# Branch projections of a conv/gMLP/MoE step in split weights and inputs, with their loads and the modulation loads on one queue

## The chip, the cores and the metric

One Trainium2 chip, one core of it. The number is the device time of one execution in microseconds. Three runs of the kernel before took 975.2, 977.08 and 981.87 us; the median is 977.08.

The engines, as the profile names them: PE (TensorE, matrix products; PEld is its weight load), DVE (VectorE), ACT (ScalarE), POOL (GpSimd), SP (SyncE, which here only issues DMAs; SPq is its DMA queue).

## The reference, cut to what matters

One inference step of one layer for 512 prompt tokens and 32 sample tokens (T = 544 together), model width D = 1024, all float32.

```
mod = silu(c) @ w_ada + b_ada            # 6 vectors of D: sh1 sc1 g1 sh2 sc2 g2
h = rms_norm(x) * (1 + sc1) + sh1
z = h @ w_in + b_in                      # conv input a (2D), u, v (D each), gates (2D)
a = silu(layer_norm(depthwise_conv(glu(a))));   y_a = a @ w_a
v = layer_norm(gelu(v));   y_b = (gelu(u) * (w_s mixes v over positions)) @ w_b
m = sigmoid(gate_a) * y_a + sigmoid(gate_b) * y_b
x = x + g1 * (m @ w_o)
h2 = rms_norm(x) * (1 + sc2) + sh2;   x = x + g2 * experts(h2);   final norm with its own mod
```

The change is in `y_b`, `y_a` (two products of 544 x 1024 by 1024 x 1024) and in what is loaded from there to the output projection.

## The kernel before

Everything is one program with one instruction stream per engine, written out by hand; semaphores order the streams. In most stages the activations lie transposed: 128 channels on the partitions, the 544 tokens along the row, 8 such tiles for D (`KT` = 8).

**Stages.** Conv input and v projection; u projection (`U_U`, 4 units); gates (`U_G`, 8 units, 16 output tiles); branch projections (`U_YB`, `U_YA`; 16 output tiles, the first 8 are `uT` by w_b, the other 8 `aT` by w_a); output projection (`U_O`); routing; experts. The weights of all these go through two buffers of 16 KB a partition, `W[0]` and `W[1]`, used in turn. The same two places are called `WP[s]` when a unit of only 2 x 128 output columns is loaded; then `wH2[s]` and `wL2[s]` are its halves. `w_used` counts the units that TensorE has finished, `w_full` the loads that landed.

**Two kinds of product.** `product` (L511 to L518) gives one output tile of 128 x 544: for each of 8 k, two float32 matmuls of 272 columns; in the trace each of these is two records. `product_split` (L577 to L583) gives the same tile from operands split in two parts, each in the type float32r: high (the value rounded to it) and low (the rest). It makes three products for each k: high weights by high input, high by low, low by high; 48 matmuls of 272 columns, each one record. The u projection and the gates are done so, the branch projections in `product`.

**Who splits.** ScalarE copies the weights of a unit to `wH2` (`high_of`, L961 to L964). POOL subtracts that from the weights (`low_gate`, L1631 to L1634; VectorE does it for the u projection) and writes `wL2`, over the place of the loaded weights. `gH`, `gL` are the split input of the gates; `gL` lies where `x` lay (`O_X`).

**Branch stage.** For output tile j, TensorE waits for the weights (`full`) and for the PSUM banks that merge(j-2) has drained, then makes `product`. VectorE's `merge(j)` (L1307 to L1322) multiplies the result by a gate and, for j >= 8, adds it to the first branch in `mT`. In between, TensorE makes 12 small products of the conditioning with 512 columns of w_ada or w_ada_f (`ada(m)`, L684 to L693, after tile m + 3), each from a 2 MB load into `AW[m % 2]`. VectorE's `add_bias(m)` (L1324 to L1333) sums four partial rows and the bias, POOL writes the row to `mod` in HBM and loads the bias row of m + 2. ada(m) waits for add_bias(m-2). POOL issues all these loads (`load_mod`, `load_bias`).

**SP's queue.** It loads the units in order, each when `w_used` frees its buffer; between w_b and w_a it loads `x` a second time, since L1359 adds to it. After w_o it loads the vectors g1, sc2 (`g1b`, `a2b`), g_norm2 (`gn2b`), sh2 (`sh2b`) and then the first experts' weights.

**Output projection.** TensorE makes token blocks 0 and 1 with the first half of w_o, then waits for the second half (L726 and on). VectorE (L1342 to L1368) multiplies by g1, adds x, norms and modulates to h2, which TensorE transposes block by block.

Of the kernel before, what the change touches and what calls it, by code (L numbers as in the profile page):

```python
# [31 lines left out]
P = 128  # L32
D = 1024
# [38 lines left out]
def build(nc, a, y_out, hist_p_out, hist_s_out, v_out):  # L72
    with ExitStack() as ctx:
# [21 lines left out]
        gH, gL = split_parts("gH", O_S, KT, T), split_parts("gL", O_X, KT, T)  # L95
        wH2 = [split_parts(f"wH2{s}", O_W + 4096 * s + 2048, 2, KT, P) for s in range(2)]
# [130 lines left out]
        x2_in = sem("x2_in")  # L227
        u_split = sem("u_split")
        bias_split, conv_sum = sem("bias_split"), sem("conv_sum")
# [146 lines left out]
        U_A, U_V, U_U, U_G, U_YB, U_YA, U_O = 4, 12, 14, 18, 26, 28, 30  # L376
# [3 lines left out]
        NB = 12  # L380
# [18 lines left out]
        def _(sp):  # L399
# [11 lines left out]
            def unit_load(n, cols):  # L411
                sp.wait_ge(w_used, n - 1 if n >= U_A + 2 else n - 3)
                for m in range(2):
                    sp.dma_start(WP[n % 2][:, m], w_in[:, :, cols[m]:cols[m] + P]).then_inc(w_full[n % 2], 16)
# [21 lines left out]


            for p in range(2):
                sp.wait_ge(mod_stored[p], 16 * 3)
            for s, rows in ((0, P), (1, NSAMPLE)):  # L440
                g_rows = P if s == 0 else 2 * NSAMPLE
                sp.dma_start(g1b[s][0:g_rows, :], mod_vec(2, g_rows, s)).then_inc(mb_in, 16)
                sp.dma_start(a2b[s][0:rows, :], mod_vec(4, rows, s)).then_inc(mb_in, 16)
            sp.wait_ge(mod_added, NB)
            sp.dma_start(gn2b, a["g_norm2"].to_broadcast([P, D])).then_inc(mb2_in, 16)
            sp.wait_ge(dve_drained, KT + NGATE)
            for s, rows in ((0, P), (1, NSAMPLE)):
                sp.dma_start(sh2b[s][0:rows, :], mod_vec(3, rows, s)).then_inc(mb2_in, 16)

# [60 lines left out]
        def _(pe):  # L510
# [66 lines left out]
            def product_split(bank, w_high, w_low, act_high, act_low):  # L577
# [121 lines left out]
            for j in range(NGATE):  # L699
                n = U_YB + j // 4  # L700
                if j % 4 == 0:
                    full(pe, n)
                if j == KT:
                    pe.wait_ge(a_ready, 2 * KT)
                if j >= 2:
                    pe.wait_ge(dve_drained, KT + j - 1)
                last = product(2 * (j % 2), W[n % 2][:, :, (j % 4) * P:(j % 4 + 1) * P], uT if j < KT else aT)
                last.then_inc(w_used if j % 4 == 3 else y_ps, 1)
# [178 lines left out]
        def _(act):  # L887
# [237 lines left out]
        def _(dve):  # L1125
# [180 lines left out]

            def merge(j):  # L1307
                b, n = j % 2, U_YB + j // 4
                m_j = two(mT[:, j % KT, :])
                if j % 4 == 3:  # L1310
                    dve.wait_ge(w_used, n + 1)
                else:
                    dve.wait_ge(y_ps, 3 * (j // 4) + j % 4 + 1)
# [35 lines left out]
            for t in range(TT):  # L1349
# [8 lines left out]
                dve.wait_ge(o_drained, 2 * t + 2)  # L1358
                dve.tensor_tensor(x[0:w, t, :], x[0:w, t, :], mg[0:w, :], ALU.add).then_inc(x1_ready, 1)  # L1359
# [3 lines left out]
                if t >= 2:  # L1363
# [3 lines left out]
                                              op0=ALU.mult, op1=ALU.mult))  # L1367
                dve.tensor_tensor(h2[0:w, t % 2, :], h2[0:w, t % 2, :], sh2b[s][0:w, :], ALU.add).then_inc(h2_ready, 1)  # L1368
# [230 lines left out]
        def _(pool):  # L1599
# [55 lines left out]
            def mod_of(m):  # L1655
                return (w_ada, a["b_ada"], (4 + m) * BLK) if m < 8 else (w_adaf, b_adaf, (m - 8) * BLK)

            def load_mod(m):
                src, bias, c0 = mod_of(m)
                pool.dma_start(AW[m % 2], src[:, :, c0:c0 + BLK]).then_inc(mod_in[m % 2], 16)  # L1660

            def load_bias(m):
                src, bias, c0 = mod_of(m)
                pool.dma_start(brow[:, m % 2, :], bias[:, c0:c0 + BLK].to_broadcast([2, BLK])).then_inc(bias_in[m % 2], 16)

# [89 lines left out]
```

## Time and profile before

| | |
|---|---|
| median of three runs | 977.08 us |
| profiled execution | 976.06 us, its span 974.3 us |
| PE busy | 862.8 us, 89% of the span |
| DVE, ACT, POOL busy | 495.0, 168.1, 150.1 us |
| branch products and adas | 415.2 to 557.5 us |
| output projection | from 559.2 us |

The span is what the profiler saw from first to last instruction; some 1.8 us lie around it. "Busy" of PE counts matmuls, which overlap each other, so full means that it always had one in work, not that it ran at its peak. PEclk is the clock granted to TensorE as a share of 2.4 GHz: 1.00 is 2.4, 0.50 is 1.2. An idle time in brackets at the end of a timeline row stands before the instruction and names what ended it.

### The profile page before, as it was taken

How to read it: one execution, taken by the hardware profiler on the slowest of the kernel's cores; microseconds unless marked ns; L12 is line 12 of the kernel's file. 1: busy time of each engine (PE TensorE's matmuls, PEld its weight loads, DVE VectorE, ACT ScalarE, POOL GpSimd, SP SyncE). 2: the span in 40 equal slices, each digit the busy share in tenths (PEclk: the TensorE clock that was granted, in tenths of full speed). 3: DMA queues.
4: the chain of work that ended last, by engine and by line, in shares of the span. 5: the costliest groups of instructions: out<-in, count | busy, mean ns of one | idle time of the engine just before them, and what ended most of it. 6: DMA issues, size and time to landing. Idle time of an engine off the chain costs nothing. (4 is left out here: it accounts for less than half of the span.)

```text
span 974.3 us, 11529 instructions
## 1 busy us (share of the span) xinstructions
PE 862.8 (89%) x4738; PEld 613.3 (63%) x4738; DVE 495.0 (51%) x734; ACT 168.1 (17%) x255; POOL 150.1 (15%) x176
## 2 busy tenths in 40 slices
PE   2899999999997979899999999926999996979776
PEld 1588886347996979877666644524666664545432
DVE  1429999999999543301434425472333332222226
ACT  3211211111232121800000012100211110101003
POOL 1000000000056273201112000001222222121110
PEclk9899999999998889999999999955999998999889
DMA  9913214012323124275778392162899999999926
GB/s 321 326 47 87 80 50 173 1 43 66 90 67 96 39 55 153 102 264 196 261 276 307 101 385 99 48 259 76 357 397 419 418 415 390 374 408 396 379 105 255
DMA packets 94709, 204.12 MB, mean 210 GB/s; under 512 B 10028, under 2 KB 52372, under 8 KB 86462
## 3 DMA queue, kind: packets, MB, share of 16 engines
q1 hardware_dynamic: 69200, 134.10, 37.9%
q0 software_dynamic: 12624, 34.32, 9.6%
q10 hardware_dynamic: 12830, 34.93, 9.3%
q8 instruction: 39, 0.64, 0.3%
q14 instruction: 16, 0.13, 0.0%
HBM read 199.49 MB, written 14.84 MB: 220 GB/s over the span
## 5 line engine op out<-in xcount | busy, mean ns | idle before, releaser
L517 PE MATMUL PS<-arena 128*128 128x272 f32 x1024 | 240.9, 397 | 3.5 <-issue 1.9
L517 PEld LDWEIGHTS PS<-arena 128*128 128x128 f32 x1024 | 195.0, 191 | 53.8 <-issue 13.8
L1236 DVE SCALAR_TENSOR_TENSOR arena<-arena,VT 128x574 f32<-128x574 f32 x240 | 175.2, 818 | 0.0
L824 PE MATMUL PS<-arena 128*64 128x256 f32 (+1 forms) x1056 | 148.2, 410 | 29.9 <-issue 25.8
L824 PEld LDWEIGHTS PS<-arena 128*64 128x64 f32 (+1 forms) x1056 | 108.1, 156 | 65.4 <-issue 38.7
L582 PE MATMUL PS<-gH,wH 128*128 128x272 f32 x384 | 82.1, 296 | 9.2 <-POOL wL L1634 5.6
L1634 POOL TENSOR_TENSOR wL<-arena,wH 128x1024 fp32r<-128x1024 f32 x16 | 40.9, 2582 | 271.1 <-ACT wH L964 271.1
L582 PE MATMUL PS<-gL,wH 128*128 128x272 f32 x384 | 81.2, 293 | 0.0
L582 PE MATMUL PS<-gH,wL 128*128 128x272 f32 x384 | 80.9, 292 | 0.0
L1530 DVE TENSOR_TENSOR arena<-PS,arena 128x256 f32<-128x256 f32 x19 | 8.1, 425 | 139.5 <-ACT arena L1070 139.5
L844 PE MATMUL PS<-arena 128*64 128x512 f32 (+1 forms) x264 | 69.1, 597 | 1.4 <-DVE arena L1534 1.4
L582 PEld LDWEIGHTS PS<-gH,wH 128*128 128x128 f32 x384 | 61.4, 193 | 11.2 <-POOL wL L1634 5.8
L582 PEld LDWEIGHTS PS<-gH,wL 128*128 128x128 f32 x384 | 61.9, 193 | 0.0
L582 PEld LDWEIGHTS PS<-gL,wH 128*128 128x128 f32 x384 | 61.6, 193 | 0.0
L1710 POOL DMA_INDIRECT pairs<-arena,sidx x19 | 30.6, 1613 | 191.4 <-DVE arena L1546 191.4
L718 PE MATMUL PS<-arena 128*128 128x512 f32 x128 | 55.5, 593 | 1.7 <-DVE arena L1322 1.7
L619 PE MATMUL PS<-arena 128*128 128x512 f32 x128 | 56.2, 592 | 0.0
L1050 ACT ACTIVATE tmp<-arena 128x1024 f32<-128x1024 f32 (+1 forms) x6 | 6.3, 1058 | 222.1 <-DVE arena L1359 202.8
L844 PEld LDWEIGHTS PS<-arena 128*64 128x64 f32 (+1 forms) x264 | 22.6, 145 | 34.0 <-issue 32.5
L718 PEld LDWEIGHTS PS<-arena 128*128 128x128 f32 x128 | 24.1, 190 | 31.2 <-issue 31.2
L1070 ACT ACTIVATE arena<-PS 128x256 f32<-128x256 f32 x19 | 7.3, 385 | 209.1 <-PE PS L824 209.1
L619 PEld LDWEIGHTS PS<-arena 128*128 128x128 f32 x128 | 24.3, 190 | 29.0 <-issue 28.8
(275 smaller groups left out, 811.3 us busy)
## 6 DMA issues: line engine op xcount, KB each, us to landing
arena<-w_gate SPq DMA_DIRECT2D x32, 1024.0 KB
arena<-w_up SPq DMA_DIRECT2D x32, 1024.0 KB
arena<-w_down ACTq DMA_DIRECT2D x28, 1024.0 KB, 15.5
arena<-w_in SPq DMA_DIRECT2D x40, 512.0 KB, 5.2
arena<-w_ada SPq DMA_DIRECT2D x4, 2048.0 KB, 20.6
vecs<-w_ada POOLq DMA_DIRECT2D x4, 2048.0 KB, 9.5
arena<-w_ada POOLq DMA_DIRECT2D x4, 2048.0 KB, 8.5
arena<-x_prompt SPq DMA_DIRECT2D x8, 512.0 KB, 10.5
```

The lines of the kernel that those rows point to most:

```text
L517: last = pe.matmul(PS[:, bank + h, 0:H], tile_w[:, k, :], act[:, k, h * H:(h + 1) * H], start=(k == 0), stop=(k == KT - 1))
L582: last = pe.matmul(PS[:, bank + h, 0:H], w[:, k, :], part[:, k, h * H:(h + 1) * H], start=(k == 0 and n == 0), stop=(k == KT - 1 and n == 2))
L619: last = pe.matmul(PS[:, bank, :], hT[:, k, t * P:(t + 1) * P], W[hf][:, k, :], start=False, stop=(k == KT - 1))
L718: last = pe.matmul(PS[:, (2 * t + hf) % 8, :], mT[:, k, t * P:(t + 1) * P], W[hf][:, k, :], start=(k == 0), stop=(k == KT - 1))
L824: last = pe.matmul(PS[h * rows:(h + 1) * rows, 2, n * DE:(n + 1) * DE], hG[:, b, k * SLOTS + h * rows:k * SLOTS + (h + 1) * rows], buf[r / ...
L844: last = pe.matmul(PS[h * rows:(h + 1) * rows, 4 + 2 * b + hf, :], heT[:, k, h * rows:(h + 1) * rows], WD[r // 2][r % 2][:, k, hf * 512:(h ...
L1050: act.activation(scratch[0:w, :], src, ACT.Square, accum_out=ss[0:w, t:t + 1]).then_inc(act_step, 1)
L1070: act.activation(sil, PS[:, 2, 0:DE], ACT.Silu).then_inc(sil_ready, 1)
L1236: dve.scalar_tensor_tensor(out=total, in0=src, scalar=tap, in1=total, op0=ALU.mult, op1=ALU.add).then_inc(conv_step, 1)
L1530: dve.tensor_tensor(he, PS[:, 2, DE:2 * DE], sil, ALU.mult).then_inc(he_ready, 1)
L1634: pool.tensor_tensor(wL2[q % 2][:, m], WP[q % 2][:, m], wH2[q % 2][:, m], ALU.subtract).then_inc(gw_split, 1)
L1710: pool.indirect_dma_start(out=pairs, out_offset=bass.IndirectOffsetOnAxis(ap=sidx[b][:, 0:1], axis=0), in_=Y[:, b, :], in_offset=None, bou ...
```

## The change

The branch projections are made with `product_split`. Their weights come in 8 units of 256 columns instead of four halves of 512; units are split by ScalarE and POOL as in the gates (POOL's `low_gate` now runs to unit 16). The inputs are split too: `yH` is the high part (at `O_X`, where `gL` was), `uL` and `aL` are written over `uT` and `aT`. For u the first three high parts are copied by VectorE, the other five by ScalarE; for a all eight by ScalarE. VectorE makes the low parts; those of a stand before merge(7) in its stream. TensorE waits per k for them in tiles 0 and 8. ScalarE's `high_of(U_YB)` stands before the last two gate drains. All modulation and bias loads and the `mod` stores move from POOL's queue to SP's, among the unit loads. g1 and sc2 are loaded within the branch stage; x (whose place yH now has) after the second half of w_o, its parts each with the semaphore of its first load, VectorE waiting per token block; sh2 is waited for only at the first block's last step.

```diff
+        yH, uL, aL = split_parts("yH", O_X, KT, T), split_parts("uL", O_U, KT, T), split_parts("aL", O_C, KT, CONV)
...
-        U_A, U_V, U_U, U_G, U_YB, U_YA, U_O = 4, 12, 14, 18, 26, 28, 30
+        U_A, U_V, U_U, U_G, U_YB, U_YA, U_O = 4, 12, 14, 18, 26, 30, 34
-        NB = 12
+        NB, EARLY = 12, 3
...
-            for n, (src, c0) in enumerate(((w_b, 0), (w_b, BLK))):
-                half_load(U_YB + n, src, c0)
-            for t in range(4):
-                sp.dma_start(x[:, t, :], a["x_prompt"][0, t * P:(t + 1) * P, :]).then_inc(x2_in, 16)
-            sp.dma_start(x[0:NSAMPLE, 4, :], a["x_sample"][0]).then_inc(x2_in, 16)
-            for n, (src, c0) in enumerate(((w_a, 0), (w_a, BLK), (w_o, 0), (w_o, BLK))):
-                half_load(U_YA + n, src, c0)
+            def branch_load(q):
+                unit_load(U_YB + q, [(2 * (q % 4) + m) * P for m in range(2)], w_b if q < 4 else w_a)
...
+            branch_load(0)
+            branch_load(1)
+            sp.wait_ge(gated, KT)
+            load_mod(0)
+            sp.wait_ge(w_used, U_YB)
+            load_mod(1)
+            load_bias(0)
+            load_bias(1)
+            for j in range(NGATE):
+                if j % 2 == 1 and j // 2 + 2 < 8:
+                    branch_load(j // 2 + 2)
+                if 3 <= j < 3 + NB - 2:
+                    sp.wait_ge(mod_ps, j - 2)
+                    load_mod(j - 1)
+                if 4 <= j < 4 + NB:
+                    m = j - 4
+                    sp.wait_ge(mod_added, m + 1)
+                    sp.dma_start(mod[:, (4 + m) * BLK:(5 + m) * BLK], mrow[:, m % 2, :]).then_inc(mod_stored[m % 2], 16)
+                    if m + 2 < NB:
+                        load_bias(m + 2)
+                if j == 12:
...
+                if j == 13:
+                    half_load(U_O, w_o, 0)
+            sp.dma_start(gn2b, a["g_norm2"].to_broadcast([P, D])).then_inc(gn_in, 16)
+            half_load(U_O + 1, w_o, BLK)
+            for t in range(2):
+                sp.dma_start(x[:, t, :], a["x_prompt"][0, t * P:(t + 1) * P, :]).then_inc(x_in[t], 16)
             sp.wait_ge(dve_drained, KT + NGATE)
...
...
                 for k in range(KT):
+                    if split is not None:
+                        pe.wait_ge(y_split, split + k + 1)
...
             for j in range(NGATE):
-                n = U_YB + j // 4
-                if j % 4 == 0:
-                    full(pe, n)
-                if j == KT:
-                    pe.wait_ge(a_ready, 2 * KT)
+                q, m = j // 2, j % 2
+                pe.wait_ge(gw_split, NGATE + j + 1)
                 if j >= 2:
                     pe.wait_ge(dve_drained, KT + j - 1)
-                last = product(2 * (j % 2), W[n % 2][:, :, (j % 4) * P:(j % 4 + 1) * P], uT if j < KT else aT)
+                last = product_split(2 * m, wH2[q % 2][:, m], wL2[q % 2][:, m], yH, uL if j < KT else aL, j if j % KT == 0 else None)
...
+            high_of(U_YB)
             gate(NGATE - 2)
             gate(NGATE - 1)
+            for j in range(EARLY, KT):
+                act.activation(yH[:, j, :], uT[:, j, :], ACT.Copy).then_inc(y_high, 1)
+            for n in range(1, 5):
+                high_of(U_YB + n)
+            act.wait_ge(w_used, U_YA)
+            for j in range(KT):
+                act.activation(yH[:, j, :], aT[:, j, 0:T], ACT.Copy).then_inc(y_high, 1)
+            for n in range(5, 8):
+                high_of(U_YB + n)
...
+            def low_of(first, before, src, dst):
+                for j in range(first, KT):
+                    dve.wait_ge(y_high, before + j - first + 1)
+                    dve.tensor_tensor(dst[:, j, 0:T], src[:, j, 0:T], yH[:, j, :], ALU.subtract).then_inc(y_split, 1)
...
+            dve.wait_ge(gated, KT)
+            dve.wait_ge(w_used, U_YB)
+            for j in range(EARLY):
+                dve.tensor_copy(yH[:, j, :], uT[:, j, :]).then_inc(y_copied, 1)
+                dve.wait_ge(y_copied, j + 1)
+                dve.tensor_tensor(uL[:, j, 0:T], uT[:, j, 0:T], yH[:, j, :], ALU.subtract).then_inc(y_split, 1)
+            low_of(EARLY, 0, uT, uL)
             dve.wait_ge(gate_drained, NGATE)
             for j in range(NGATE):
+                if j == KT - 1:
+                    dve.wait_ge(a_ready, 2 * KT)
+                    low_of(0, KT - EARLY, aT, aL)
                 merge(j)
...
-            dve.wait_ge(x2_in, 16 * TT)
             dve.wait_ge(mb_in, 64)
-            dve.wait_ge(mb2_in, 48)
+            dve.wait_ge(gn_in, 16)
...
+                dve.wait_ge(x_in[t], 32)
+                if t == 0:
+                    dve.wait_ge(mb2_in, 32)
...
-            for q in range(4, 8):
+            for q in range(4, 16):
                 low_gate(q)
...
```

## Rows read from the trace of the kernel before

**Rows 1.** Windows: stretch, length, busy PE, PEld, DVE, ACT, POOL; PEclk, DMA share, GB/s.
```profile
415.20:557.50 142.30, 142.28 (x704) 101.09 (x704) 45.05 (x66) 0.00 (x0) 19.68 (x31) 1.00 0.65 238
...
380.00:386.00 6.00, 6.00 (x50) 6.00 (x50) 0.00 (x0) 2.57 (x3) 4.75 (x2) 1.00 0.00 0
```

**Rows 2.** Timeline of PE (start, us, line, count): branch products, adas, output projection.
```profile
415.22 10.09 PE L517 MATMUL PS<-arena 128*128 128x272 f32 x43 [1.91 <-issue]
...
444.72 1.92 PE L692 MATMUL PS<-vecs 128*32 128x512 f32 x16
...
454.11 1.92 PE L692 MATMUL PS<-arena,vecs 128*32 128x512 f32 x16
...
559.17 27.70 PE L718 MATMUL PS<-arena 128*128 128x512 f32 x64 [1.67 <-DVE arena L1322]
```

**Rows 3.** Timeline of DVE in the branch stage: two merges, add_bias's last three steps.
```profile
437.50 0.72 DVE L1316 TENSOR_TENSOR arena<-PS,arena 128x544 f32<-128x544 f32 x1 [6.61 <-PE PS L517]
444.83 0.72 DVE L1316 TENSOR_TENSOR arena<-PS,arena 128x544 f32<-128x544 f32 x1 [6.61 <-PE PS L517]
...
550.25 2.13 DVE L1331 TENSOR_TENSOR mrow<-PS,mrow 2x512 f32<-2x512 f32 x3
```

**Rows 4.** Timelines of SPq and ACT: a gate unit's load and split, gate drains.
```profile
374.08 0.99 SPq L414 DMA_DIRECT2D arena<-w_in  x2
...
379.96 2.01 ACT L964 ACTIVATE wH<-arena 128x1024 fp32r<-128x1024 f32 x2 [5.15 <-DMA arena<-w_in]
...
386.20 0.71 ACT L1006 ACTIVATE arena<-PS,VT 128x544 f32<-128x544 f32 x1 [3.63 <-PE PS L582]
...
412.40 1.28 ACT L1006 ACT_TABLE_LOAD   x1
413.69 1.32 ACT L1006 ACTIVATE arena<-PS,VT 128x544 f32<-128x544 f32 x2
```

**Rows 5.** Timelines of POOL and DVE: low weights, one DVE product beside them.
```profile
271.69 7.45 POOL L1634 TENSOR_TENSOR wL<-arena,wH 128x1024 fp32r<-128x1024 f32 x2 [246.53 <-ACT wH L964]
...
313.47 9.30 POOL L1634 TENSOR_TENSOR wL<-arena,wH 128x1024 fp32r<-128x1024 f32 x4
...
318.47 4.89 DVE L1296 TENSOR_TENSOR arena<-arena,tmp 128x544 f32<-128x544 f32 x1
...
393.08 4.75 POOL L1634 TENSOR_TENSOR wL<-arena,wH 128x1024 fp32r<-128x1024 f32 x2 [7.24 <-ACT wH L964]
```

**Rows 6.** Timeline of PE, then a window, after the longest idle gap in gates.
```profile
359.96 0.82 PE L582 MATMUL PS<-gH,wH 128*128 128x272 f32 x2 [5.56 <-POOL wL L1634]
...
362.00:364.00 2.00, 2.00 (x11) 2.00 (x11) 1.97 (x2) 0.18 (x1) 2.00 (x3) 0.52 0.03 8
```

**Rows 7.** Groups by form: count, busy us, mean ns of one.
```profile
L1242 DVE TENSOR_TENSOR gL<-arena,gH 128x544 fp32r<-128x544 f32 x8 | 5.2, 726 | 0.0
...
L960 ACT ACTIVATE gH<-arena 128x544 fp32r<-128x544 f32 x8 | 4.9, 673 | 0.0
```

**Rows 8.** Windows (columns of Rows 1); DMA issues: KB each, median us to landing.
```profile
10.00:20.00 10.00, 2.83 (x16) 0.68 (x16) 1.61 (x3) 7.04 (x12) 0.00 (x0) 1.00 1.08 338
...
366.00:368.00 2.00, 2.00 (x18) 2.00 (x18) 2.00 (x1) 0.00 (x0) 2.00 (x2) 1.00 1.02 410
...
386.00:392.00 6.00, 6.00 (x47) 5.79 (x46) 0.00 (x0) 0.77 (x2) 0.00 (x0) 1.00 0.64 175
...
vecs<-w_ada POOLq DMA_DIRECT2D x4, 2048.0 KB, 9.5
...
arena<-w_o SPq DMA_DIRECT2D x2, 1024.0 KB, 6.5
...
arena<-mod SPq DMA_DIRECT2D x2, 128.0 KB, 10.7
```

**Rows 9.** Timelines of SPq and DVE at the head of the output projection.
```profile
561.80 0.35 SPq L445 DMA_DIRECT2D arena<-g_norm  x1
...
580.04 0.69 DVE L1357 TENSOR_TENSOR tmp<-PS,arena 128x512 f32<-128x512 f32 x1 [2.55 <-PE PS L718]
```

More of the change, by code:

```diff
@@ L226, in build @@
         w_full = [sem("w_full0"), sem("w_full1")]
-        x2_in = sem("x2_in")
+        gn_in = sem("gn_in")
         u_split = sem("u_split")
+        y_high, y_copied, y_split = sem("y_high"), sem("y_copied"), sem("y_split")
         bias_split, conv_sum = sem("bias_split"), sem("conv_sum")
@@ L433, in mod_vec, with mod_of, load_mod, load_bias @@
+            def mod_of(m):
+                return (w_ada, a["b_ada"], (4 + m) * BLK) if m < 8 else (w_adaf, b_adaf, (m - 8) * BLK)
+            def load_mod(m):
+                src, bias, c0 = mod_of(m)
+                sp.dma_start(AW[m % 2], src[:, :, c0:c0 + BLK]).then_inc(mod_in[m % 2], 16)
+            def load_bias(m):
+                src, bias, c0 = mod_of(m)
+                sp.dma_start(brow[:, m % 2, :], bias[:, c0:c0 + BLK].to_broadcast([2, BLK])).then_inc(bias_in[m % 2], 16)
             def mod_vec(n, rows, s):
@@ L434, in mod_vec @@
                 return mod[s:s + 1, n * D:(n + 1) * D].to_broadcast([rows, D])
[L438 to L445, printed above, removed]
+            branch_load(0)
@@ new lines, in _ @@
+            branch_load(1)
[18 more added lines that the diff above has]
+                if j == 12:
+                    sp.wait_ge(w_used, U_YA)
+                    for p in range(2):
+                        sp.wait_ge(mod_stored[p], 16 * 3)
+                    for s, rows in ((0, P), (1, NSAMPLE)):
+                        g_rows = P if s == 0 else 2 * NSAMPLE
+                        sp.dma_start(g1b[s][0:g_rows, :], mod_vec(2, g_rows, s)).then_inc(mb_in, 16)
+                        sp.dma_start(a2b[s][0:rows, :], mod_vec(4, rows, s)).then_inc(mb_in, 16)
+                if j == 13:
+                    half_load(U_O, w_o, 0)
@@ L448, in _ @@
                 sp.dma_start(sh2b[s][0:rows, :], mod_vec(3, rows, s)).then_inc(mb2_in, 16)
+            for t in range(2, 4):
+                sp.dma_start(x[:, t, :], a["x_prompt"][0, t * P:(t + 1) * P, :]).then_inc(x_in[t], 16)
+            sp.dma_start(x[0:NSAMPLE, 4, :], a["x_sample"][0]).then_inc(x_in[4], 16)
             sp.wait_ge(hist_ps, 2)
@@ L575, in _, with product_split @@
             pe.wait_ge(ws_copied, 1)
-            def product_split(bank, w_high, w_low, act_high, act_low):
+            def product_split(bank, w_high, w_low, act_high, act_low, split=None):
                 for k in range(KT):
+                    if split is not None:
+                        pe.wait_ge(y_split, split + k + 1)
                     for n, (w, part) in enumerate(((w_high, act_high), (w_high, act_low), (w_low, act_high))):
@@ L699, in _ @@
             for j in range(NGATE):
[L700 to L704 removed]
+                q, m = j // 2, j % 2
+                pe.wait_ge(gw_split, NGATE + j + 1)
                 if j >= 2:
                     pe.wait_ge(dve_drained, KT + j - 1)
[L707 to L708 removed]
+                last = product_split(2 * m, wH2[q % 2][:, m], wL2[q % 2][:, m], yH, uL if j < KT else aL, j if j % KT == 0 else None)
+                last.then_inc(w_used if m == 1 else y_ps, 1)
                 if 3 <= j < 3 + NB:
@@ L1304, in _ @@
                 dve.tensor_tensor(cv[:, j, :], cv[:, j, :], rstdc[:, :], ALU.mult).then_inc(c_normed, 1)
+            def low_of(first, before, src, dst):
+                for j in range(first, KT):
+                    dve.wait_ge(y_high, before + j - first + 1)
+                    dve.tensor_tensor(dst[:, j, 0:T], src[:, j, 0:T], yH[:, j, :], ALU.subtract).then_inc(y_split, 1)
             def merge(j):
-                b, n = j % 2, U_YB + j // 4
+                b, n = j % 2, U_YB + j // 2
                 m_j = two(mT[:, j % KT, :])
-                if j % 4 == 3:
+                if b == 1:
                     dve.wait_ge(w_used, n + 1)
                 else:
-                    dve.wait_ge(y_ps, 3 * (j // 4) + j % 4 + 1)
+                    dve.wait_ge(y_ps, j // 2 + 1)
                 y = PS[:, 2 * b:2 * b + 2, 0:H]
@@ L1653, in _ @@
                 pool.tensor_tensor(sq[:, j, :], cv[:, j, :], cv[:, j, :], ALU.mult).then_inc(squared, 1)
[L1655 to L1664, printed above, removed]
-            for q in range(4, 8):
-                low_gate(q)
-                if q == 4:
-                    pool.wait_ge(gated, KT)
-                    load_mod(0)
-                    load_bias(0)
-                    load_bias(1)
-            pool.wait_ge(w_used, U_YB)
-            load_mod(1)
-            for m in range(NB):
-                if m + 2 < NB:
-                    pool.wait_ge(mod_ps, m + 1)
-                    load_mod(m + 2)
-                pool.wait_ge(mod_added, m + 1)
-                pool.dma_start(mod[:, (4 + m) * BLK:(5 + m) * BLK], mrow[:, m % 2, :]).then_inc(mod_stored[m % 2], 16)
-                if m + 2 < NB:
-                    load_bias(m + 2)
+            for q in range(4, 16):
+                low_gate(q)
             pool.wait_ge(tokens_known, 1)
```

4 lines of the change are left out of this document (2 added, 2 removed).

## The prediction

> **What bounds the kernel now.** I read the windows of the stage that changes first, then the timelines inside it and around its two ends. Between 415.2 and 557.5 us TensorE is busy 142.28 of 142.30 us at full clock, VectorE 45, ScalarE 0, the DMA engines 65% [rows 1]: the branch stage is bound by TensorE alone, and any saving there moves the end. The reader should see a beat in [rows 2]: one 128x544 product in full float32, then one 512-column modulation product (`ada`), every 9.39 us. Before the first ada VectorE's merges start 7.33 us apart [rows 3]. So a product costs 7.33 and an ada 2.06: 16 x 7.33 + 12 x 2.06 = 142.0, which is the stage. The gates, done as three products of split operands each, take 12.1 us a unit of two, from 374.08 (its predecessor's end lets a load go) to the drain at 386.20, so 6.06 each [rows 4], and there TensorE and its weight load are both full [rows 1].
>
> **The products.** Removed: 16 products of 7.33. Added: 16 of 48 matmuls, of the gates' own shape, at 6.06. That is 16 x 1.27 = **20.3 us** gained. Ada keeps its 2.06. 6.06 us is 126 ns a matmul, each with its own weight load, in the same instruction as the new ones will be, so I take it. The Trainium skill (TensorE: Matmul & The Clock Gate, section Back-to-back issue gap) gives a lone matmul columns over 2.4 GHz plus 2.5 ns, which for 272 columns is an estimated 116 ns; by it a product would be 5.56 us and the gain 28; the trace's gates don't agree.
>
> **Getting the weights split.** In the gates a 1 MB unit (two loads) is issued at 374.08, is in ScalarE's hands at 379.96 (5.9 later), takes 2.01 for both high parts and 4.75 for both low parts on POOL, of which TensorE waits for the first half [rows 4, 5]: 5.9 + 1.0 + 2.4 = 9.3 us. A buffer is refilled when its unit ends; the next unit covers 12.1 us without ada, 12.1 + 3 x 2.06 = 18.3 with. Both exceed 9.3, so units 1 to 7 cost nothing. If that cover went, each would cost the shortfall.
>
> **The hand-over from gates to branches, term 1.** ScalarE is done with its second group of Silu at 412.4, loads a table and drains gates 14 and 15 by 415.01; the products start 0.2 later [rows 2, 4]. The new `high_of(U_YB)` stands before those drains: +2.01. TensorE still waits for all 16 drains, so it may start at 417.2 instead of 415.2: **2.0 us** lost.
>
> **The hand-over, term 2.** gL's place becomes yH, so no high part of u can be written before the last gate ends at 413.3 (415.22 less 1.91 idle). VectorE then makes three copies and differences; in the same microseconds POOL makes the first two low weights, from 413.4 (first high part) to 418.2. A VectorE difference of this size takes 0.73 us [rows 7], but a product of that size with both inputs in SBUF, begun while POOL worked on low weights, took 4.89 and ended 0.6 after POOL's run [rows 5]. So I take the first difference as done at 418.9, not 414.8. TensorE then has been idle 5.6 us; after the idle 5.56 us before 359.96 it ran at the 1.2 GHz level to 364, 11 matmuls in two microseconds where full clock gives 18 by the same count [rows 6, 8], 0.228 us apart instead of 0.126. From 419.0 three of the eight k steps (six matmuls each) then take 1.37 and five take 0.76: 7.9 us, end 426.9. VectorE keeps ahead of this (a copy at most as long as a difference, 0.73, and differences 5.2 / 8 = 0.65 apart), and ScalarE's five copies at 4.9 / 8 = 0.61 from 417.0 are ready by 420.1 [rows 7]. Without either effect product 0 would end at 423.3: **3.6 us** lost. Bounds: 0 (POOL and VectorE miss each other) and 6.3 (POOL takes 7.45 for its pair beside a busy VectorE, as once [rows 5]). Early copies on VectorE thus buy little; ScalarE's come soon after.
>
> **The middle.** At product 8 the same yH is refilled from aT. ScalarE starts when product 7 ends (T), VectorE's first difference is ready at T + 1.5, ada(4) covers until T + 2.06, and eight differences 0.65 apart stay ahead of k steps of 0.76 [rows 7]. But merge(7) and add_bias(3) now stand behind the eight differences: merge ends near T + 6.8, add_bias, four steps of 2.13 / 3 [rows 3], at T + 9.6. ada(5) needs it at T + 8.1: **1.5 us** lost. Bounds 0 and 4. Later a merge's second step (two SBUF inputs) can meet POOL's low weights: at most 4.2 late, against a slack of 8.1 - 4.4 = 3.7, so under half a microsecond for each of three units; I count nothing.
>
> **The loads.** All adas and biases move from POOL's queue to SP's, in one order with the units. SP waits for product end, ada end, add_bias end, in the order in which these happen, so no wait holds up an earlier need. Per two products: one unit and two 2 MB ada loads, 5.24 MB in 16.2 us, 323 GB/s. A backlogged queue moved 338 GB/s at the kernel's start and 410 in an ada load alone, so 2 MB are 5.2 us; in the six microseconds of a unit's load the DMA engines were busy 0.64, 3.8 us [rows 8]. So 3.8 + 2 x 5.2 = 14.2 of 16.2 us: tight, but it fits, and an ada load has 14 us from issue to need against 9.5 to land. Bias loads and `mod` stores now sit behind a 2 MB load, some 6 us; a bias has 12 from issue to need. POOL's freed issue time had no waiter.
>
> **The output projection.** The second half of w_o was issued as the last product ended; now it stands behind add_bias(11), whose end let gn2b go 4.3 us after the products [rows 9], and behind gn2b itself. It landed 6.5 after issue; with the later issue and 0.5 MB ahead, that is end + 13.4. TensorE needs it at end + 1.7 + 27.7 / 2 = 15.5 [rows 2, 8]. Hidden with 2 us to spare; at the 10.7 of a neighbouring load it would cost 1. x is queued right behind (2.6 us for each MB) and needed only when the first row block's second half is in, 22.5 after the end [rows 9]. VectorE's wait for the vectors goes, but what is late next, the product at 580.04, bounds it, so nothing is gained. After that all is as before: the experts' first loads go out some 3 us later with over 60 to spare.
>
> **Sum.** 20.3 - 2.0 - 3.6 - 1.5 = 13.2. The profiled execution took 976.06 (span 974.3), so 962.9; the median of the three, 977.08, stands 1.0 above it. I predict **963 us**.
>
> **Rivals.** (1) Free hand-overs: only the ScalarE term stays, gain 18.3, 958 (957 if that too hides). For it: POOL may finish before VectorE asks. Against: the 4.89 us row. 0.17. (2) The matmuls follow each other faster than in the gates. A full float32 matmul is two records of 235 ns (43 in 10.09 us [rows 2]); if each is two passes, a pass of 272 columns takes 117 ns, and at that pace a product is 5.63: 7 us more, 956. Against: the gates, same shape, same engine state, keep 126. 0.03. The page named above would have it so. (3) Loads on one queue reach about 300 GB/s: 17.5 instead of 16.2 per pair, five pairs, 6 us worse, 970. For it: 65% DMA before becomes 80 to 90, and the old stage moved only 238 GB/s [rows 1]; against: it had no backlog. 0.14. (4) Slower than before: the same queue under 271 GB/s (5.24 MB per 19 us) would have each ada wait for mod_in and eat the 13.2; under about 249, 21 us per pair, it ends over 1% slower, 988 or so. It decides only if mixing 512-byte with 2 KB pieces costs a third of the rate; no row shows a backlogged queue that slow for more than a microsecond or two. 0.06. Forecast: 0.60.
>
> **Numbers.** 1% (what can be told from no change) is 9.8 us: below 967.3 is faster. Forecast with its bounds runs 959 to 968, nine tenths of it below: 0.56 + 0.17 + 0.03 = 0.76 faster; 0.04 + 0.14 = 0.18 same; 0.06 slower. The range 955 to 971 takes in rivals 1 and 2 and most of 3.
>
> **What would show it.** Products: pairs of units 16.2 us apart, sum of PE windows 20 us shorter. Term 1: last gate sigmoid near 417.0. Term 2: first VectorE difference ending near 418.9 and the clock at half in the first 4 us of products. Middle: one TensorE wait of 1.5 us for mrow before the sixth ada. Loads: no wait of TensorE for mod_in or for a low weight. It is wrong if TensorE waits on DMA in the stage, if a product is not 6.06, or if a wait appears before the second half of w_o.

## The result, and the profile after

| us | before | after |
|---|---|---|
| median of four runs each, same chip | 978.89 | 965.97 |
| lowest and highest | 975.2 to 981.87 | 963.69 to 970.1 |
| profiled execution (its span) | 976.06 (974.3) | 964.99 (963.2) |

The ratio is 0.989, 95% interval 0.9856 to 0.9923: a gain clear of noise, though the interval takes in 0.99, where the prediction drew its line for "faster". At the medians it is 12.9 us, between the two profiled executions 11.1; the forecast sum was 13.2.

Busy time in the page of the kernel after, which answers to the table before:

```profile
PE 845.6 (88%) x4994; PEld 618.5 (64%) x4994; DVE 509.0 (53%) x753; ACT 190.9 (20%) x284; POOL 168.8 (18%) x156
```

ScalarE and POOL have 22.8 and 18.7 us more, the new splits. That is little beside the stage; what they cost lies in where they stand.

**The stage.** The windows of the kernel after (stretch, length, busy PE, PEld, DVE, ACT, POOL with counts, PEclk, DMA share, GB/s) answer to [rows 1]:

```profile
429.00:545.60 116.60, 115.08 (x912) 95.90 (x911) 51.67 (x74) 16.55 (x20) 29.36 (x12) 1.00 0.80 268
```

From the end of product 0 TensorE has all but 1.5 us filled, at full clock. The merges, in the timeline of DVE (start, us, engine, line, operation, tiles, count, idle before it and what ended it), stand 6.02 apart where [rows 3] had 7.33:

```profile
435.05 0.72 DVE L1365 TENSOR_TENSOR arena<-PS,arena 128x544 f32<-128x544 f32 x1 [5.23 <-PE PS L619]
441.08 0.72 DVE L1365 TENSOR_TENSOR arena<-PS,arena 128x544 f32<-128x544 f32 x1 [5.30 <-PE PS L619]
```

**The hand-over.** The last gate product, ScalarE's tail of the gates, and product 0, in the timelines of PE, ACT, POOL and DVE. They answer to [rows 2, 4, 5]:

```profile
406.23 0.49 PE L619 MATMUL PS<-gH,wH 128*128 128x272 f32 x2 [1.76 <-ACT arena L1040]
...
411.46 1.99 ACT L998 ACTIVATE wH<-arena 128x1024 fp32r<-128x1024 f32 x2
414.76 1.32 ACT L1040 ACTIVATE arena<-PS,VT 128x544 f32<-128x544 f32 x2
...
412.58 4.87 POOL L1695 TENSOR_TENSOR wL<-arena,wH 128x1024 fp32r<-128x1024 f32 x2 [15.50 <-ACT wH L998]
420.84 5.74 POOL L1695 TENSOR_TENSOR wL<-arena,wH 128x1024 fp32r<-128x1024 f32 x2 [3.39 <-ACT wH L998]
...
414.18 1.07 DVE L1389 CAST yH<-arena 128x544 fp32r<-128x544 f32 x1 [9.64 <-PE PS L619]
415.28 2.75 DVE L1391 TENSOR_TENSOR uL<-arena,yH 128x544 fp32r<-128x544 f32 x1
420.18 7.61 DVE L1354 TENSOR_TENSOR uL<-arena,yH 128x544 fp32r<-128x544 f32 x5
...
418.18 0.79 PE L619 MATMUL PS<-yH,wH 128*128 128x272 f32 x2 [4.14 <-DVE uL L1391]
...
427.21 0.53 PE L619 MATMUL PS<-yH,wH 128*128 128x272 f32 x2 [1.55 <-DVE uL L1354]
```

Read it from above. ScalarE splits w_b first (411.46, 1.99) and so ends its drains at 416.08. POOL makes the first pair of low weights from 412.58 to 417.45. VectorE's first copy can begin when the last gate product is done, 414.04, and its first difference (2.75 instead of 0.72) ends with POOL, at 418.03. Product 0 begins at 418.18. Then the row to notice: the five differences as a block take 7.61 us where [rows 7] give 3.3, beside POOL's **second** pair, and TensorE stops for them inside product 0, ahead of its seventh k step. The same five in the view of their tile (duration in ns, min/median/max, then first and last start):

```profile
L1354 DVE TENSOR_TENSOR uL<-arena,yH x5: 710/717/2893, 420.2 to 427.1; 128x544 fp32r<-128x544 f32 x5
```

So they were not slowed evenly: three took their lone 0.72 us and two took 2.89. Those two ended at 424.34 and 427.16, each 0.58 us after one of POOL's two instructions (423.76, 426.58).

**The clock.** Windows of the same execution (columns as above), first in the last gate product, then in product 0:

```profile
408.00:410.00 2.00, 2.00 (x11) 2.00 (x10) 0.00 (x0) 2.00 (x5) 0.00 (x0) 0.50 0.00 0
...
419.00:421.00 2.00, 2.00 (x10) 2.00 (x10) 1.97 (x5) 1.30 (x2) 0.16 (x1) 0.50 1.04 380
423.00:425.00 2.00, 2.00 (x13) 2.00 (x12) 2.00 (x2) 0.00 (x0) 2.00 (x2) 0.68 1.08 416
```

After 4.14 us idle the products ran at the 1.2 GHz level until 424.2, as forecast only longer. The first window was not forecast: the last gate product, after an idle time of 1.76 us as before the change, also fell to that level, took 7.8 us instead of 6.3, and ended the gates at 414.04 though it began 0.8 earlier than before.

**The middle and the end of the stage.** Timelines of DVE and PE:

```profile
480.16 5.18 DVE L1354 TENSOR_TENSOR aL<-arena,yH 128x544 fp32r<-128x544 f32 x8 [5.36 <-ACT yH L1079]
486.71 2.13 DVE L1380 TENSOR_TENSOR mrow<-PS,mrow 2x512 f32<-2x512 f32 x3
489.63 1.80 DVE L1371 TENSOR_TENSOR arena<-arena,tmp 128x544 f32<-128x544 f32 x1
...
488.98 1.92 PE L729 MATMUL PS<-arena,vecs 128*32 128x512 f32 x16 [1.52 <-DVE mrow L1380]
...
547.34 13.11 PE L752 MATMUL PS<-arena 128*128 128x512 f32 x30 [1.67 <-DVE arena L1371]
```

merge(7), 0.72, and add_bias(3) (to 488.84) stand behind the eight differences, and the sixth ada waits 1.52 us for them. A later merge's second step took 1.80 us instead of 0.73 beside POOL, and TensorE waited for none of these. The last product ends at 545.67. In the stage no wait of TensorE names a DMA.

**The loads.** DMA issues of the kernel after (KB each, median us from issue to landing), against [rows 8]:

```profile
vecs<-w_ada SPq DMA_DIRECT2D x4, 2048.0 KB, 9.3
arena<-w_b SPq DMA_DIRECT2D x8, 512.0 KB, 4.5
arena<-w_o SPq DMA_DIRECT2D x4, 1024.0 KB, 7.0
```

A window over one full beat of the stage, two products and two adas (columns as above):

```profile
497.20:513.40 16.20, 16.20 (x132) 13.02 (x134) 8.37 (x13) 2.01 (x2) 5.21 (x2) 1.00 0.96 325
```

TensorE has no gap in it, and the DMA engines have almost none either: 0.96, where the prediction's 14.2 of 16.2 us is 0.88.

From the first product of the output projection to the end of the span it is 415.8 us, 415.1 before.

### The profile page after: what moved, and what is told of

Its sections match the earlier page's. It is cut to its first block and busy times, and to the rows that moved or that the text cites. A ratio compares the mean times of both kernels' runs of the same rounds, so it can differ in the third digit from the quotient of the medians.

```text
span 963.2 us, 12133 instructions
## 1 busy us (share of the span) xinstructions
PE 845.6 (88%) x4994; PEld 618.5 (64%) x4994; DVE 509.0 (53%) x753; ACT 190.9 (20%) x284; POOL 168.8 (18%) x156
## 5 line engine op out<-in xcount | busy, mean ns | idle before, releaser
L858 PEld LDWEIGHTS PS<-arena 128*64 128x64 f32 (+1 forms) x1056 | 108.8, 156 | 65.4 <-issue 36.9
L1695 POOL TENSOR_TENSOR wL<-arena,wH 128x1024 fp32r<-128x1024 f32 x32 | 83.2, 2621 | 360.8 <-ACT wH L998 360.8
L552 PE MATMUL PS<-arena 128*128 128x272 f32 x512 | 119.1, 396 | 1.6 <-DVE arena L1242 1.6
L552 PEld LDWEIGHTS PS<-arena 128*128 128x128 f32 x512 | 98.3, 192 | 22.1 <-issue 1.6
L998 ACT ACTIVATE wH<-arena 128x1024 fp32r<-128x1024 f32 x40 | 40.1, 1051 | 125.9 <-DMA arena<-w_in 50.8
L619 PE MATMUL PS<-yH,wH 128*128 128x272 f32 x256 | 55.5, 299 | 5.7 <-DVE uL L1391 4.1
L619 PE MATMUL PS<-yH,wL 128*128 128x272 f32 x256 | 53.9, 292 | 0.0
L619 PEld LDWEIGHTS PS<-yH,wH 128*128 128x128 f32 x256 | 41.2, 194 | 16.2 <-issue 10.2
```

The source lines that it names most:

```text
L552: last = pe.matmul(PS[:, bank + h, 0:H], tile_w[:, k, :], act[:, k, h * H:(h + 1) * H], start=(k == 0), stop=(k == KT - 1))
L858: last = pe.matmul(PS[h * rows:(h + 1) * rows, 2, n * DE:(n + 1) * DE], hG[:, b, k * SLOTS + h * rows:k * SLOTS + (h + 1) * rows], buf[r / ...
L998: act.activation(wH2[n % 2][:, m], WP[n % 2][:, m], ACT.Copy).then_inc(gw_high, 1)
L1695: pool.tensor_tensor(wL2[q % 2][:, m], WP[q % 2][:, m], wH2[q % 2][:, m], ALU.subtract).then_inc(gw_split, 1)
```

## The experiments

Each was timed with runs of the kernel before on its chip. The first four share one chip (before: median 977.8 of 9 runs), the last four another (977.1 of 17). Ratios are to the kernel before.

| | median us | runs | ratio | 95% |
|---|---|---|---|---|
| the changed kernel again | 968.69 | 5 | 0.9911 | 0.9897 to 0.9925 |
| POOL waits | 963.65 | 4 | 0.9862 | 0.9847 to 0.9877 |
| no early copies | 961.99 | 5 | 0.9845 | 0.9821 to 0.9868 |
| Silu later | 959.44 | 5 | 0.9815 | 0.9802 to 0.9828 |
| loads alone | 976.48 | 12 | 0.9995 | 0.9972 to 1.0018 |
| four banks | 965.06 | 6 | 0.9867 | 0.9829 to 0.9906 |
| three edits together | 954.68 | 6 | 0.9755 | 0.9724 to 0.9787 |
| filler | 959.98 | 5 | 0.9829 | 0.9796 to 0.9862 |

My theory after the result: what is missing from the forecast lies in the hand-over, where POOL's second pair holds VectorE's differences. The rival: it is the half clock alone, so only more work or less idle time on TensorE helps.

**The changed kernel again**, unchanged, as the base on that chip.

> The changed kernel once more, as the measure for the others of this chip. Theory: ratio to the kernel before 0.987 to 0.991 (0.9890 measured). In the trace: first difference of u ends near 418, product 0 ends near 429, one wait of 1.5 us before the sixth ada. Rival, that the first profile caught an unusual execution: product 0 within 12 us of the last gate instead of 15.

Its profiled execution lost more in the same place. Timelines of PE and DVE:

```profile
424.94 0.52 PE L619 MATMUL PS<-yH,wH 128*128 128x272 f32 x2 [1.08 <-DVE uL L1354]
427.75 0.52 PE L619 MATMUL PS<-yH,wH 128*128 128x272 f32 x2 [1.79 <-DVE uL L1354]
...
421.35 7.61 DVE L1354 TENSOR_TENSOR uL<-arena,yH 128x544 fp32r<-128x544 f32 x5
431.32 0.72 DVE L1365 TENSOR_TENSOR arena<-PS,arena 128x544 f32<-128x544 f32 x1 [2.37 <-PE PS L619]
```

Two stops inside product 0 instead of one. From the end of the last gate (415.20) to the start of merge(0), which stands for the end of product 0, it is 16.1 us; in the first profile (414.04 to 429.10) 15.1. VectorE is held alike in both: its block takes 7.61 us. The difference is TensorE's clock. In the first profile the half clock lasted until 424.2, and TensorE was too slow to meet the first of the two held differences. Here it was at full clock from 422.2, stopped for both, and behind the second stop fell to half clock once more (PEclk 0.50 in the window 430 to 432), so that the last two k steps took 3.6 us (427.75 to 431.32) instead of 1.9 (427.21 to 429.10).

**POOL waits.** POOL's second pair only after all eight differences.

```diff
             for q in range(4, 16):
+                if q == 9:
+                    pool.wait_ge(y_split, KT)
                 low_gate(q)
```

> The changed kernel, but POOL waits with the low weights of branch unit 1 until VectorE has made all eight low parts of u. Theory (VectorE is held by POOL's second pair of low weights, 420.8 to 426.6, and TensorE waits 1.55 us at k = 5 for it): VectorE's five differences take 3.3 us instead of 7.6, TensorE's wait within product 0 is gone, product 0 ends 1.5 to 2 us sooner, the kernel is 1.5 to 2 us shorter (ratio to the changed kernel 0.998). Unit 1's low weights are needed 12 us later and cost nothing. Rival (the wait comes from ScalarE's copies or the clock): no difference in VectorE's durations, same time.

Timelines of DVE, POOL and PE:

```profile
412.85 2.59 DVE L1389 CAST yH<-arena 128x544 fp32r<-128x544 f32 x1 [8.09 <-PE PS L619]
420.37 3.26 DVE L1354 TENSOR_TENSOR uL<-arena,yH 128x544 fp32r<-128x544 f32 x5
426.14 0.72 DVE L1365 TENSOR_TENSOR arena<-PS,arena 128x544 f32<-128x544 f32 x1 [2.51 <-PE PS L619]
...
423.70 4.73 POOL L1695 TENSOR_TENSOR wL<-arena,wH 128x1024 fp32r<-128x1024 f32 x2 [6.07 <-DVE uL L1354]
...
406.45 0.49 PE L619 MATMUL PS<-gH,wH 128*128 128x272 f32 x2 [1.62 <-ACT arena L1040]
418.37 0.79 PE L619 MATMUL PS<-yH,wH 128*128 128x272 f32 x2 [5.66 <-DVE uL L1391]
```

The block of five is back at 3.26 us, and no stop is left in product 0; POOL's later pair makes nothing late (next merge 5.95 us on). From gate end (412.71) to product 0's end 13.4 us. At the medians it is 5.0 us faster than the changed kernel, where 1.5 to 2 were expected. In the traces 2.7 of it is the hand-over (16.1 to 13.4) and 1.5 the last gate product, which ran at full clock here (6.26 us). That product ends before POOL's added wait begins, so its 1.5 us is not shown to come from the edit. The rest is the other terms together and within the scatter of single executions. For the hand-over the theory holds. The half clock was there too (PEclk 0.50 at 418 to 420), so the rival falls as the sole cause.

**No early copies.** ScalarE makes all eight high parts of u.

```diff
-NB, EARLY = 12, 3
+NB, EARLY = 12, 0
```

> The changed kernel with EARLY = 0: all eight high parts of u by ScalarE, after its two gate drains, none by VectorE. Theory (the first difference ends near 418 because POOL holds VectorE until 417.5, whoever made the high part): the first difference again ends near 418.0 and TensorE starts then; five more ScalarE microseconds move nothing that TensorE waits for, except the high weights of unit 1 by 1.8 us; within 0.5 us of the changed kernel. Rival (VectorE's early copies pay as meant): TensorE starts the products 1.5 us or more later and the kernel is 1 to 3 us longer.

Timelines of ACT, DVE, POOL and PE:

```profile
417.29 4.48 ACT L1074 ACTIVATE yH<-arena 128x544 fp32r<-128x544 f32 x8
...
418.07 5.51 DVE L1354 TENSOR_TENSOR uL<-arena,yH 128x544 fp32r<-128x544 f32 x8 [12.21 <-ACT yH L1074]
427.17 0.72 DVE L1365 TENSOR_TENSOR arena<-PS,arena 128x544 f32<-128x544 f32 x1 [3.59 <-PE PS L619]
...
422.79 5.39 POOL L1695 TENSOR_TENSOR wL<-arena,wH 128x1024 fp32r<-128x1024 f32 x2 [4.25 <-ACT wH L998]
...
419.28 0.79 PE L619 MATMUL PS<-yH,wH 128*128 128x272 f32 x2 [5.46 <-DVE uL L1354]
```

I had the copies as worth little either way, and expected a change within 0.5 us. They **cost**: without them the kernel is 6.7 us faster at the medians, of which the traces put 2.8 in the hand-over (16.1 to 13.35), 1.5 in the last gate product and 1.5 behind the start of the output projection (416.3 to 414.8). Only the 2.8 is shown to be theirs. Product 0 begins no later: 5.46 us after the gates, with copies and POOL waiting 5.66 (the 4.15 of the changed kernel follows a last gate product that was 1.5 slow). But ScalarE reaches the second unit's high parts later, POOL follows at 422.79, and most differences are done by then: gate end (413.82) to product 0's end 13.35 us, the same as with POOL waiting. Again the last gate product ran at full clock. Two different edits that both part the differences from the second pair give the same 13.4, so the mechanism is shown twice.

**Silu later.** ScalarE splits w_b before the last four convolution tiles' Silu groups are done: `high_of(U_YB)` behind the drain of gate 13, and the second four tiles' Silu behind the second unit's high parts. In outline, with `swish_a(h)` for the Silu of four tiles:

```diff
             gate(KT + 4)
             swish_a(0)
             gate(KT + 5)
-            swish_a(1)
             high_of(U_YB)
             gate(NGATE - 2)
             gate(NGATE - 1)
             ...                     # five high parts of u
             high_of(U_YB + 1)
+            swish_a(1)
```

> The changed kernel with ScalarE's stream reordered: the second four Silu of a stand after the high weights of unit 1 instead of before the last two gate drains. So the high weights of unit 0 are made while gates 14 and 15 are computed, POOL's low weights of unit 0 are done before the last gate ends, and the last drain follows the last gate. Theory (the hand-over costs what ScalarE's drain, POOL's hold on VectorE and the clock after a 4 us gap cost together): TensorE's gap between gates and products falls from 4.1 to about 1.6 us, bounded by one VectorE copy and difference, the clock stays at 2.4 GHz more often, and the kernel is 4 to 6 us shorter (ratio to the changed kernel 0.995). Rival (the gap is bound by VectorE's copies themselves): gap stays over 3 us, gain under 1.5 us.

Timelines of POOL, DVE and PE:

```profile
406.01 4.75 POOL L1699 TENSOR_TENSOR wL<-arena,wH 128x1024 fp32r<-128x1024 f32 x2 [10.04 <-ACT wH L998]
...
411.54 0.44 DVE L1393 CAST yH<-arena 128x544 fp32r<-128x544 f32 x1 [8.11 <-PE PS L619]
414.88 3.26 DVE L1358 TENSOR_TENSOR uL<-arena,yH 128x544 fp32r<-128x544 f32 x5
419.92 0.73 DVE L1369 TENSOR_TENSOR arena<-PS,arena 128x544 f32<-128x544 f32 x1 [1.77 <-PE PS L619]
...
412.89 0.49 PE L619 MATMUL PS<-yH,wH 128*128 128x272 f32 x2 [1.49 <-DVE uL L1395]
```

A window of product 0:

```profile
414.00:416.00 2.00, 1.91 (x13) 1.69 (x14) 1.97 (x4) 0.89 (x2) 0.00 (x0) 1.00 1.18 309
```

Now POOL's first pair is done before the gates end, copy and difference have their lone times, the idle time is 1.49 us and the clock stays at 2.4 GHz. Product 0 ends 8.5 us after the gates. Against POOL waits (13.4) that is 4.9 us in the traces and 4.2 at the medians. It takes away term 1 and term 2 together, and so shows their sum (5.6 forecast), not their shares. Against the changed kernel it is 9.2 at the medians, where 4 to 6 were expected; in the traces 7.6 of it is the hand-over (16.1 to 8.5) and 1.5 the last gate product.

**Loads alone.** The kernel before with nothing but the new order of loads on SP's queue. In outline:

```diff
 # POOL's stream: loads of w_ada, w_ada_f, biases, stores of mod taken out
 # SP's stream, between the unit loads
+            for j in range(2 * KT):
+                ...                 # load_mod(m), load_bias(m), store of mod(m)
+            # g1, sc2; then g_norm2, w_o half 2, x, sh2, x by blocks
```

> The kernel before, with only the loads of the change: modulation and bias loads and mod stores on SP's queue in the change's order, g1 and sc2 within the branch stage, the second half of w_o after the last add_bias and g_norm2, x after it, VectorE waiting for x per block. The branch products stay full float32 and the weights come in four halves. Theory (the order has slack everywhere): ratio to the kernel before 1.000, within 0.002; no TensorE wait for mod_in or the second half of w_o. Rival (one queue costs, or the vectors' order gains): TensorE waits in the branch stage or the output projection, 3 us or more longer; or shorter by 1 us or more.

The window over its products reads as [rows 1]:

```profile
416.00:558.00 142.00, 142.00 (x704) 101.00 (x704) 45.06 (x66) 0.00 (x0) 0.00 (x0) 1.00 0.69 247
```

0.9995 with an interval of 0.2% to each side: the order of loads neither gives nor takes. This kernel still loads w_b and w_a in rows of 2 KB, so what their 512-byte rows do to the queue is seen in the changed kernel alone, in the window above.

**Four banks.** ada(m) writes PSUM bank 4 + m % 4 instead of 4 + m % 2, and so waits for add_bias(m-4).

```diff
-                if m >= 2:
-                    pe.wait_ge(mod_added, m - 1)
+                if m >= 4:
+                    pe.wait_ge(mod_added, m - 3)
```

> The changed kernel with the modulation products in four PSUM banks instead of two, so that ada(m) waits for add_bias(m-4). Theory (the 1.5 us wait before the sixth ada is add_bias(3) standing behind eight differences): the wait is gone, 1.5 us shorter (ratio to the changed kernel 0.998). Rival (the delay only moves to the next thing that VectorE is late with): a wait of about the same length at product 9 or 10, same time.

Waits of TensorE between 412 and 555 us (engine, what it waited for, total, times, longest):

```profile
PE PS L619 <- DVE uL L1391: 4.2, 1, 4.2
PE PS L619 <- DVE uL L1354: 2.6, 2, 1.8
```

The wait for mrow is gone. From merge(0) to the output projection it took 117.48 us, in the repeat of the changed kernel 118.83, so 1.35 less. The two kernels are alike here: both stopped twice in product 0, the second time for 1.77 and 1.79 us, and fell to the lower clock once more behind it. A window of the four banks kernel:

```profile
430.00:432.00 2.00, 2.00 (x11) 2.00 (x10) 0.72 (x1) 0.00 (x0) 0.00 (x0) 0.50 0.50 182
```

The medians can't show it: 965.06, with an interval of 0.9829 to 0.9906.

**Filler.** POOL waits, and nine matmuls of 272 columns behind the last gate product, into a bank that nothing reads.

```diff
+            for k in range(9):
+                pe.matmul(PS[:, 6, 0:H], ident[:, :], tmp[:, 0, 0:H], start=True, stop=True)
```

> The kernel in which POOL waits for u's low parts, with nine matmuls of 272 columns into an unused bank right behind the last gate, 4.1 us of TensorE work that nothing reads. Theory (TensorE's clock falls to 1.2 GHz in the 5 us gap, and product 0 then pays 1.6 to 2.7 us): the clock stays at 2.4 GHz into product 0, which ends 1.6 to 2.7 us sooner, the kernel is as much shorter than without the filler. Rival (product 0 is paced by VectorE's differences at either clock): the clock stays up, but product 0 ends at most 0.5 us sooner.

Windows, and then timelines of DVE and PE:

```profile
414.00:416.00 2.00, 2.00 (x9) 1.33 (x7) 1.97 (x2) 1.99 (x5) 2.00 (x2) 1.00 1.14 321
418.00:420.00 2.00, 1.88 (x13) 1.44 (x12) 1.97 (x4) 2.00 (x3) 0.00 (x0) 1.00 1.04 397
```

```profile
417.32 0.43 DVE L1391 CAST yH<-arena 128x544 fp32r<-128x544 f32 x1
424.57 0.72 DVE L1367 TENSOR_TENSOR arena<-PS,arena 128x544 f32<-128x544 f32 x1 [1.77 <-PE PS L619]
...
417.54 0.49 PE L619 MATMUL PS<-yH,wH 128*128 128x272 f32 x2 [1.55 <-DVE uL L1393]
```

The clock stays at 1.00 through the hand-over. From the end of the first difference to merge(0) it is 7.2 us (417.40 to 424.57), with POOL waiting but no filler 7.9 (418.22 to 426.14): the half clock costs 0.7 us there. By rate it would be 1.4: with POOL waiting it lasted some 3.15 us (PEclk 0.50 at 418 to 420, 0.62 at 420 to 422), and a matmul takes 0.228 instead of 0.126. The rest is hidden, because for the first k steps VectorE's copy and difference set the pace, 1.11 us for both together: at full clock TensorE made only 13 matmuls from 418 to 420, where the windows filled by it have 18. By the traces, then, the gain lies between the rival's 0.5 and the theory's 1.6: the theory's price was too high. The medians (959.98, with POOL waiting alone 963.65) were taken on different chips, and the intervals of their ratios overlap, so they don't settle it.

**Three edits together.** Silu later with all eight groups behind the second high parts, POOL waits, four banks; product 0's first tile waits for 15 drains, not 16.

> The changed kernel with: all eight Silu of a after the hand-over, high weights of unit 0 before the last two drains, product 0 waiting for 15 drains instead of 16, POOL's low weights of unit 1 after u's low parts, four banks for the modulation products. Theory: as the reordered stream (9 us under the changed kernel), minus 1.5 for the middle, minus 1.5 to 1.8 for the wait before gate 15, which ScalarE's late drain of gate 13 causes: 956 us, ratio to the kernel before 0.978. Rival (the waits overlap and the gains don't add): no shorter than the reordered stream alone, 959.

Timeline of PE, and TensorE's waits between 400 and 555 us:

```profile
414.62 0.49 PE L619 MATMUL PS<-yH,wH 128*128 128x272 f32 x2 [1.48 <-DVE uL L1397]
```

```profile
PE PS L754 <- DVE arena L1377: 1.7, 1, 1.7
PE PS L619 <- DVE uL L1397: 1.5, 1, 1.5
```

Two waits are left, 1.5 and 1.7 us; no run put other work of TensorE in front of them. It is the fastest kernel here, 954.68 us where 956 was expected, 0.9755 of the time before, and beats the changed kernel too: its interval ends at 0.9787, that kernel's begin at 0.9856 and 0.9897. From merge(0) to the output projection it took 116.64 us, with Silu later alone 118.22: the middle's 1.5 again. The idle time before the last gate product is gone too.

## Why the prediction was right, and where its terms were off

The forecast, 963 us with 955 to 971, holds both medians of the changed kernel, 965.97 and 968.69. Term by term:

- **The products, 20.3: right.** 6.02 us apart where 6.06 was taken. After product 0 fifteen products, twelve adas and the middle wait took 116.7 us (429.0 to 545.67), forecast 117.4. At full clock the new matmuls again follow each other by 126 ns. The Trainium skill (TensorE: Matmul & The Clock Gate, Back-to-back issue gap) gives 5.6 us for a product, an estimate from its formula for an isolated matmul; the same section says that a stream of weight loads and matmuls is set by both. The new products' 6.02, as the gates' 6.06, is longer than the isolated figure.
- **Term 1, 2.0: right.** The group before the drains took 1.99, the last drain ended 9.85 us after the last gate product began (406.23 to 416.08), before 7.98. It lay under term 2, since VectorE was later still.
- **Term 2, 3.6: mis-sized, and the step that failed is one that cost nothing in my sum.** The first part holds: with the last gate at full clock (POOL waits), product 0 began 5.66 us after the gates, 5.6 forecast, and with POOL kept off its end came 13.4 after them, 13.6 forecast. But I wrote "VectorE keeps ahead of this" and "units 1 to 7 cost nothing", and asked of the second unit only whether TensorE would wait for *it*. Its low weights are made from 420.84, in the very microseconds of VectorE's differences, and TensorE waits for those. I had used the row in which POOL holds a product of two SBUF inputs for the first pair and not for the second. Price, against the 13.4: 1.6 us in the first profile, 2.7 in the repeat, part of which is the second fall of the clock behind the stop. The other units did cost nothing.
- **"Early copies on VectorE thus buy little": wrong in sign.** They begin product 0 no sooner, and let ScalarE and POOL reach the second unit 2 us sooner, into VectorE's block.
- **The half clock, inside term 2: its share over-priced.** It lasted 6.1 us in the first profile, 2.9 in the repeat and 3.15 with POOL kept off, 4 forecast. The sum priced it at 1.8 us (three k steps of 1.37 instead of 0.76); the filler shows 0.7. What fills the gap is VectorE's copy and difference, 1.11 us for each of the first k steps: it keeps ahead of k steps of 1.37, as forecast, but not of 0.76, and so product 0 took 7.0 us at full clock too (filler 417.54 to 424.57, Silu later 412.89 to 419.92). The sum is not hurt by it, since it has product 0 at half clock, 7.9 us, and with POOL waiting it took 7.8.
- **The middle, 1.5: right**, 1.52 in the trace, gone with four banks. That later merges meet POOL for nothing: right.
- **Loads and output projection, 0: right.** Loads alone 0.9995. But the second half of w_o was closer than forecast: its two pieces were issued from 550.68, the later one took 9.0 us (the four pieces of w_o took 5.0 to 9.0, median 7.0) and landed at 560.13, 14.5 us after the products, with 1.0 to spare before the 15.5. The forecast's 13.4 took a median over pieces, 6.5, where the last piece counts; before the change that one landed 8.2 after the first issue.
- **Not in the sum: 1.5 us in the last gate product**, which ran at 1.2 GHz in both profiles of the changed kernel and in four banks, and at full clock in the kernel before and the six others. Sorted by the idle time in front of it, the full ones had 1.48, 1.62, 1.66, 1.71, 1.73 and 1.76 us, the half ones 1.76, 1.81 and 1.92 (with three edits together it had none, and full clock). That fits the length of the idle time, with 1.76 on both sides; what makes it some tenths longer in these three I did not find, and no run was made for it. It stays open.

So 13.2 forecast, 11.1 measured: 0.7 from the last gate (1.5 slower, begun 0.8 earlier), 1.4 from term 2, 0.7 back from the stage, and 0.7 behind it (415.8 for 415.1), which over all profiles varies from 413.8 (loads alone) to 416.5. In the repeat the gain at the medians was 9.1 us (977.8 to 968.69), with the larger price in the hand-over.

Of the rivals, free hand-overs (958) is what Silu later comes to, so the price of the hand-over was real and was one of order. Matmuls at 117 ns did not occur. The two on the queue fell: TensorE waited for no DMA, and the beat of 16.2 us kept its 325 GB/s. But it was tighter than the 268 GB/s and 80% over the whole stage suggest: in that beat the share was 0.96, with less room than the 14.2 of 16.2 us that was forecast.

## What to carry to other kernels

When an edit splits operands on the fly, list for the first microseconds who runs beside whom, not only who waits for whom: a producer that is itself in time can hold the engine that is not. Before giving an idle engine part of a job to be early, ask what the relieved engine does next and whom that meets. And at a stage boundary, move the work that nobody waits for behind the work that feeds TensorE: here that was worth 9.2 us at the medians (968.69 to 959.44), 7.6 in the hand-over by the traces and 1.5 in the last gate product, whose clock is not explained; the sum had booked 5.6 as the price of the hand-over.

## What the runs showed of the hardware that was not expected

- **VectorE beside POOL, by kind.** A difference of two SBUF inputs took 0.72 us alone, 2.75 beside POOL's differences, and a copy with one SBUF input, which I had taken at the length of a lone difference, 0.44 alone and 2.59 beside them (POOL waits and filler). POOL itself lost less: 4.75 became at most 5.74 for a pair. The loss looks like a wait and not like a lower rate: in all profiles with the split products the VectorE instructions of two SBUF inputs that took longer beside POOL ended 0.58 to 0.59 us after a POOL instruction (418.03, 424.34 and 427.16 after 417.45, 423.76 and 426.58 in the changed kernel), and the held copies 0.30 after one (415.44 after 415.14 with POOL waiting). So it depends on where within POOL's 2.4 us VectorE comes: the same copy took 1.07 or 2.59. The Trainium skill (GPSIMD Engine Reference, Specifications) says that GpSimd shares its SBUF interfaces with VectorE, with contention for instructions in a 2-port mode or with two SBUF inputs. The traces agree on the two inputs; the copy would be the other case, and in which mode it ran no row shows.
- **The lower clock after a short stop.** The granted clock fell to 0.50 behind idle times of 1.76, 1.81 and 1.92 us ahead of the last gate product and of 1.77 and 1.79 inside product 0, and not behind six others of 1.48 to 1.76 ahead of the last gate product, nor behind 1.55 inside product 0. It fell about 1 us after TensorE had begun again. Behind 1.49 us ahead of product 0, and in the 5.67 us there with nine filler matmuls in them, it stayed at 1.00.
- **One queue for everything.** 512-byte and 2 KB pieces mixed on SP's queue: 0.5 MB landed 4.5 us after issue, 2 MB 9.3. With an ada load alone it moved 410 GB/s at a DMA share of 1.05 (window 510 to 512 of the changed kernel); with a unit's 512-byte pieces among them 307 at a share of 1.20 (500 to 502). So the queue's rate goes by what is in it, and the sum was right to price the two apart (5.2 us for 2 MB, 3.8 for a unit).
